# Attention with one head between its steps: minima of head h, then normalising h-1, scores of h+1, then turning h-1

## The chip, the cores and the metric

The kernel runs on one core of one Trainium2 chip. The metric is the device time of one execution in microseconds (us), lower is better. A core has TensorE (PE, matrix products; its weight loads are listed as PEld), VectorE (DVE), ScalarE (ACT), GpSimd (POOL) and SyncE (SP). Each engine takes its own instructions in the order in which they are written; engines wait for one another by semaphores, counters that one raises and another waits on.

## What is computed

A trunk of two residual layers over 512 tokens of width 1024, in float32. Layer 0 mixes tokens by a short gated convolution, layer 1 by multi-head latent attention; behind each mixer stands a SwiGLU feed-forward network, and a final RMS norm ends it. The change touches the attention of layer 1 alone: 16 heads, four blocks of 128 queries, and block j sees the first (j+1)*128 keys.

```python
for j in range(s // Q_BLOCK):
    q0, q1 = j * Q_BLOCK, (j + 1) * Q_BLOCK
    kend = q1
    logits = (jnp.einsum('bqhd,bkhd->bhqk', q_nope[:, q0:q1], k_nope[:, :kend])
              + jnp.einsum('bqhr,bkr->bhqk', q_rope[:, q0:q1], k_rope[:, :kend]))
    logits = logits.astype(jnp.float32) * scale
    mask = (pos[None, :kend] // CHUNK) <= (pos[q0:q1, None] // CHUNK)
    logits = jnp.where(mask[None, None], logits, NEG_INF)
    p = jax.nn.softmax(logits, axis=-1).astype(v.dtype)
    outs.append(jnp.einsum('bhqk,bkhd->bqhd', p, v[:, :kend]))
o = jnp.concatenate(outs, axis=1).reshape(bsz, s, MLA_HEADS * MLA_V)
return o @ w_o
```

## The kernel before

The program is written engine by engine, each with its own list of steps; nothing reorders them. The whole sequence stays on chip, transposed (features on partitions). Products of weights are made of three float32r products (high by high, high by low, low by high, lines 375 to 377). The stages follow one another: convolution, feed-forward, latent projections, attention, its output projection `mla_out`, feed-forward, final norm.

Within attention every head h goes through these steps:

- `q_head(h)` on TensorE makes the queries (6 products) and `rotate(h)` on VectorE applies the rotary table and writes them to `q_even` or `q_odd`. Both run ahead of the heads and end with head 15.
- `logits(h)` on TensorE (line 1552): scores of the four query blocks, into PSUM banks 0, 2 and 1, in three groups, each of which raises `s_prod`. There is one set of banks, so each group of `logits(h)` waits until `row_low(h-1)` has read its bank (`s_read`).
- `row_low(h)` on VectorE (line 1256): four instructions that scale and mask the scores, write them to `prob` and give each row's minimum of the negated score. `prob` has two buffers, by the head's parity, and so `row_low(h)` waits for `turn(h-2)` to be complete (`p_turned` at 3*(h-2)+3).
- `exponentials(h, 0)` and `(h, 1)` on ScalarE (line 852): exponentials in place, with sums of rows, for blocks 3 and 1, then 2 and 0 (`exp_done`).
- `normalise(h)` on VectorE (lines 1268 and 1272): reciprocals of the sums, and `prob` times them, for the same two halves. It ends with `p_ready`.
- `turn(h)` on TensorE (line 1613): ten transposes of 128x128 into PSUM banks 3 to 5. It waits for `p_ready` of h and, since those banks are single, for the copies of head h-1 (`pt_front`, `pt_back`).
- `front_copy(h)` on ScalarE (lines 861 and 863, two copies) and `back_copies(h)` on VectorE (line 1280, one copy) bring the transposed probabilities to SBUF, into `prob_T` or `prob_T2` by parity.
- `weigh(pair)` on TensorE (line 1629): 16 products with the values, for two heads at once; then `head_out(pair)` on ScalarE (line 867) and on VectorE (line 1284) splits the pair's output into `hid_hi` and `hid_lo`.

Two pieces of the next stage lie in between: `unit_hi` on ScalarE (line 350) and `unit_lo` on VectorE (line 359) split the first four weight blocks of `mla_out`, one in each pair 3 to 6.

The order is written by hand and goes by pairs i = 1 to 7. TensorE: logits(2i), turn(2i-1), logits(2i+1), weigh(i-1), turn(2i). VectorE: row_low(2i), back_copies(2i-1), normalise(2i), row_low(2i+1), normalise(2i+1), head_out(i-1), back_copies(2i). Here the minima of a head and its normalising stand next to each other on VectorE, while ScalarE makes the exponentials in between. After the pairs TensorE waits for the last `s_read` and goes on with products of `mla_out` over the finished chunks, with turn(15) and weigh(7) between them.

Of the kernel before, what the change touches and what calls it, by code (L numbers as in the profile page):

```python
# [91 lines left out]
def trunk_kernel(nc, w, consts, out):  # L92
# [7 lines left out]
    HEADS, NOPE, ROPE, VD = 16, 64, 32, 64  # L100
# [5 lines left out]
    PAIRS = HEADS // 2  # L106
# [24 lines left out]
    with ExitStack() as ctx:  # L131
# [211 lines left out]
        def unit_hi(eng, name, i, u):  # L343
            v, s, prev, nth = unit_numbers(name, i, u)
            _, n, width = source(name, i, u)
            eng.wait_ge(raw_in[s], nth * 16)
            if prev is not None:
                wait(eng, w_used, prev + 1)
            for dst, src in split_parts(name, s, n, width, wgt_hi):
                ins = nc.scalar.activation(dst, src, ACT.Copy)  # L350
            ins.then_inc(w_hi, 1)

        def unit_lo(eng, name, i, u):
            v, s, prev, nth = unit_numbers(name, i, u)
            _, n, width = source(name, i, u)
            wait(eng, w_hi, v + 1)
            for (dst, src), (hi, _) in zip(split_parts(name, s, n, width, wgt_lo),
                                           split_parts(name, s, n, width, wgt_hi)):
                ins = nc.vector.tensor_tensor(dst, src, hi.bitcast(F32), ALU.subtract)  # L359
            ins.then_inc(w_lo, 1)  # L360
# [284 lines left out]
        def _(sc):  # L645
# [200 lines left out]
            def exponentials(hd, n):  # L846

                par = hd % 2
                sc.wait_ge(s_read, 3 * hd + n + 2)
                for j in ((3, 1), (2, 0))[n]:  # L850
                    blk = prob[:, par, L_OFF[j]:L_OFF[j] + (j + 1) * P]
                    ins = nc.scalar.activation(blk, blk, ACT.Exp, bias=low[:, par, j:j + 1], scale=-1.0,
                                               accum_out=sums[:, par, j:j + 1])
                ins.then_inc(exp_done, 1)

            def front_copy(hd):

                sc.wait_ge(p_turned, 3 * hd + 1)
                if hd >= 2:
                    sc.wait_ge(pv_done, hd // 2)  # L860
                nc.scalar.activation(prob_Ts[hd % 2][:, 0, 0:512], ps[:, 3, :], ACT.Copy)
                sc.wait_ge(p_turned, 3 * hd + 3)
                nc.scalar.activation(prob_Ts[hd % 2][:, 0, 512:1024], ps[:, 4, :], ACT.Copy).then_inc(pt_front, 1)

            def head_out(pair):
                sc.wait_ge(pv_done, pair + 1)
                nc.scalar.activation(hid_hi[:, pair, :], ps[:, 6 + pair % 2, :], ACT.Copy).then_inc(o_hi, 1)

            exponentials(0, 0)
            exponentials(0, 1)  # L870
            exponentials(1, 0)
            exponentials(1, 1)
            front_copy(0)
            for i in range(1, PAIRS):
                exponentials(2 * i, 0)
                front_copy(2 * i - 1)
                exponentials(2 * i, 1)
                if 3 <= i < 7:
                    unit_hi(sc, "mla_out", 0, i - 3)
                exponentials(2 * i + 1, 0)  # L880
                exponentials(2 * i + 1, 1)
                head_out(i - 1)
                front_copy(2 * i)
            front_copy(HEADS - 1)
            head_out(PAIRS - 1)

# [36 lines left out]
        def _(ve):  # L923
# [313 lines left out]
            def rotate(hd):  # L1237

                if hd % GROUP == GROUP - 1:
                    ve.wait_ge(w_used, U0["q_up"] + hd // GROUP + 1)  # L1240
                else:
                    ve.wait_ge(q_prod, q_count(hd))
                nc.vector.tensor_tensor(q_Ts[hd % 2][:, hd // 2, :], ps[:, 6 + hd % 2, :], rope[:, :],
                                        ALU.mult).then_inc(q_out, 1)

            def row_low(hd):

                par = hd % 2
                if hd >= 2:
                    ve.wait_ge(p_turned, 3 * (hd - 2) + 3)  # L1250
                for n, j in enumerate((3, 1, 2, 0)):
                    W = (j + 1) * P
                    if n < 3:
                        ve.wait_ge(s_prod, 3 * hd + n + 1)
                    bank, col = {3: (0, 0), 1: (2, 0), 2: (1, 0), 0: (1, 384)}[j]
                    ins = nc.vector.tensor_tensor_reduce(
                        prob[:, par, L_OFF[j]:L_OFF[j] + W], ps[:, bank, col:col + W], mask[:, S - W:S],
                        -SCALE, 3.0e38, ALU.add, ALU.min, low[:, par, j:j + 1])
                    if n != 2:
                        ins.then_inc(s_read, 1)  # L1260

            def normalise(hd):

                par = hd % 2
                for n, js in enumerate(((3, 1), (2, 0))):
                    ve.wait_ge(exp_done, 2 * hd + n + 1)
                    two = slice(js[1], js[0] + 1, 2)
                    nc.vector.reciprocal(rec[:, par, two], sums[:, par, two]).then_inc(rec_done, 1)
                    ve.wait_ge(rec_done, 2 * hd + n + 1)
                    for j in js:  # L1270
                        blk = prob[:, par, L_OFF[j]:L_OFF[j] + (j + 1) * P]
                        ins = nc.vector.tensor_scalar(blk, blk, rec[:, par, j:j + 1], None, ALU.mult)
                ins.then_inc(p_ready, 1)

            def back_copies(hd):

                if hd >= 2:
                    ve.wait_ge(pv_done, hd // 2)
                ve.wait_ge(p_turned, 3 * hd + 2)
                nc.vector.tensor_copy(prob_Ts[hd % 2][:, 0, 1024:1280], ps[:, 5, 0:256]).then_inc(pt_back, 1)  # L1280

            def head_out(pair):
                ve.wait_ge(o_hi, pair + 1)
                nc.vector.tensor_tensor(hid_lo[:, pair, :], ps[:, 6 + pair % 2, :], hid_hi[:, pair, :].bitcast(F32),
                                        ALU.subtract).then_inc(o_lo, 1)
# [6 lines left out]
            for hd in range(3, 8):  # L1292
                rotate(hd)
            row_low(0)
            rotate(8)
            rotate(9)
            normalise(0)
            rotate(10)
            row_low(1)
            rotate(11)  # L1300
            normalise(1)
            back_copies(0)
            rotate(12)
            rotate(13)
            for i in range(1, PAIRS):
                row_low(2 * i)
                if i == 1:
                    rotate(14)
                back_copies(2 * i - 1)
                normalise(2 * i)  # L1310
                if i == 1:
                    rotate(15)
                row_low(2 * i + 1)
                if 3 <= i < 7:
                    unit_lo(ve, "mla_out", 0, i - 3)
                normalise(2 * i + 1)
                head_out(i - 1)
                back_copies(2 * i)
            back_copies(HEADS - 1)
            head_out(PAIRS - 1)  # L1320

# [44 lines left out]
        def _(pe):  # L1366
# [236 lines left out]
            def turn(hd):  # L1603

                pe.wait_ge(p_ready, hd + 1)
                if hd:
                    pe.wait_ge(pt_front, hd)
                    pe.wait_ge(pt_back, hd)
                for bs in ((0,), (2,), (1, 3)):
                    for b in bs:  # L1610
                        bank, col = {0: (3, 0), 2: (5, 0), 1: (4, 0), 3: (4, 384)}[b]
                        for j in range(b, TB):
                            ins = nc.tensor.transpose(ps[:, bank, col + (j - b) * P:col + (j - b + 1) * P],
                                                      prob[:, hd % 2, L_OFF[j] + b * P:L_OFF[j] + (b + 1) * P], ident)
                    ins.then_inc(p_turned, 1)
# [30 lines left out]
                q_head(hd)  # L1646
            logits(1)
            q_head(11)
            turn(0)
            q_head(12)  # L1650
            q_head(13)
            for i in range(1, PAIRS):
                logits(2 * i)
                if i == 1:
                    q_head(14)
                turn(2 * i - 1)
                if i == 1:
                    q_head(15)
                logits(2 * i + 1)
                weigh(i - 1)  # L1660
                turn(2 * i)

            def mla_out_products(u, ks):

# [1 line left out]
                chunk_products("mla_out", 0, u, ks, o_lo, 0)  # L1666

            pe.wait_ge(s_read, 3 * HEADS)
            mla_out_products(0, list(range(6)))
            turn(HEADS - 1)  # L1670
            mla_out_products(0, [6])
            mla_out_products(1, early)
            weigh(PAIRS - 1)
            mla_out_products(2, early)
            for u in range(3):
# [100 lines left out]
```

## Time and profile before

| | us |
|---|---|
| median of 3 runs | 1130.08 |
| lowest, highest | 1127.64, 1130.85 |
| the profiled execution, its own time | 1127.99 |
| its span in the profile | 1126.0 |
| TensorE busy | 1081.3 (96% of the span) |
| VectorE busy | 855.9 (76%) |
| ScalarE busy | 485.1 (43%) |

The profile is of one execution; times within it count from the start of the span, and 2.0 us of the execution's own time lie outside the span. Busy time of TensorE is modelled at the ends of products, which overlap a little; starts of instructions are the safer reading. "Idle before" is the time in which an engine stood still ahead of an instruction, with what ended it.

### The profile page before, as it was taken

To read this page: it belongs to the slowest core of one execution; us is meant where nothing else is said; L and a number is where in the kernel's file an instruction comes from. 1 tells how busy PE (TensorE), PEld (TensorE's weight loads), DVE (VectorE), ACT (ScalarE), POOL (GpSimd) and SP (SyncE) were. 2 spreads that over 40 slices of the span, in tenths; PEclk is the share of its full clock that TensorE was granted. 3 is DMA by queue.
4 is the path that set the end of the run, shared out by engine and by line. 5 is a ranking of instruction groups with operands and counts; after the bars stand their busy time and mean duration, and the time that the engine had idled before them with its cause. 6 is when DMAs were issued, how large, how long until landed. Compare 5 with 4: busy or idle time off the path is not lost. (4 is left out here: it accounts for less than half of the span.)

```text
span 1126.0 us, 19245 instructions
## 1 busy us (share of the span) xinstructions
PE 1081.3 (96%) x6630; PEld 956.1 (85%) x6630; DVE 855.9 (76%) x1316; ACT 485.1 (43%) x836; POOL 234.9 (21%) x179
## 2 busy tenths in 40 slices
PE   9999997799999999999999999977999999999997
PEld 7888886799999998888877766757999999988887
DVE  5855568899999997444578788388999999973443
ACT  6222233545445545222345577235454445452222
POOL 6000014333233320111200000143332333201110
PEclk9999999799999999999999999997999999999998
DMA  7333422123323333334232011021333233333321
GB/s 197 106 93 93 126 61 75 60 92 112 111 81 115 110 100 112 103 102 114 94 94 75 1 39 38 1 75 52 99 112 102 85 113 111 101 115 103 98 69 75
DMA packets 144040, 101.68 MB, mean 90 GB/s; under 512 B 3912, under 2 KB 142336, under 8 KB 144000
## 3 DMA queue, kind: packets, MB, share of 16 engines
q1 hardware_dynamic: 143648, 100.61, 29.2%
q0 software_dynamic: 320, 0.55, 0.2%
q8 instruction: 22, 0.36, 0.1%
q14 instruction: 18, 0.15, 0.0%
q10 hardware_dynamic: 32, 0.01, 0.0%
HBM read 99.06 MB, written 2.10 MB: 90 GB/s over the span
## 5 line engine op out<-in xcount | busy, mean ns | idle before, releaser
L375 PE MATMUL ps<-x_op_hi,op_w_hi 128*128 128x256 f32 x1232 | 353.5, 287 | 23.0 <-DVE x_op_lo L1021 22.1
L376 PE MATMUL ps<-x_op_lo,op_w_hi 128*128 128x256 f32 x1232 | 350.9, 285 | 0.0
L377 PE MATMUL ps<-x_op_hi,op_w_lo 128*128 128x256 f32 x1232 | 350.9, 285 | 0.0
L375 PEld LDWEIGHTS ps<-x_op_hi,op_w_hi 128*128 128x128 f32 x1232 | 239.0, 194 | 26.4 <-DVE x_op_lo L1021 22.5
L376 PEld LDWEIGHTS ps<-x_op_lo,op_w_hi 128*128 128x128 f32 x1232 | 239.0, 194 | 0.6 <-issue 0.5
L377 PEld LDWEIGHTS ps<-x_op_hi,op_w_lo 128*128 128x128 f32 x1232 | 238.9, 194 | 0.0
L375 PE MATMUL ps<-hid_hi,wgt_hi 128*128 128x512 f32 (+1 forms) x550 | 212.3, 386 | 4.2 <-DVE wgt_lo L359 4.2
L359 DVE TENSOR_TENSOR wgt_lo<-raw,wgt_hi 128x1024 fp32r<-128x1024 f32 (+4 forms) x131 | 137.6, 1066 | 101.9 <-ACT wgt_hi L350 100.5
L377 PE MATMUL ps<-hid_hi,wgt_lo 128*128 128x512 f32 (+1 forms) x550 | 210.1, 382 | 0.0
L376 PE MATMUL ps<-hid_lo,wgt_hi 128*128 128x512 f32 (+1 forms) x550 | 210.1, 382 | 0.0
L350 ACT ACTIVATE wgt_hi<-raw 128x1024 fp32r<-128x1024 f32 (+4 forms) x131 | 107.0, 831 | 151.0 <-PE ps L377 149.4
L595 POOL TENSOR_TENSOR sq<-xT 128x512 f32 (+1 forms) x36 | 38.2, 1062 | 560.4 <-DVE xT L1009 320.6
L510 DVE TENSOR_TENSOR op_w_lo<-w_sum,op_w_hi 128x512 fp32r<-128x512 f32 x176 | 135.2, 787 | 0.0
L505 ACT ACTIVATE op_w_hi<-w_sum 128x512 fp32r<-128x512 f32 x176 | 106.7, 623 | 66.1 <-PE ps L377 27.3
L610 POOL TENSOR_TENSOR w_sum<-pair_raw 128x512 f32<-128x512 f32 x44 | 68.9, 1565 | 271.6 <-DMA pair_raw<-in_ffn_w_up 145.5
L375 PEld LDWEIGHTS ps<-hid_hi,wgt_hi 128*128 128x128 f32 x550 | 103.7, 189 | 25.1 <-issue 5.4
L377 PEld LDWEIGHTS ps<-hid_hi,wgt_lo 128*128 128x128 f32 x550 | 103.8, 189 | 20.2
L376 PEld LDWEIGHTS ps<-hid_lo,wgt_hi 128*128 128x128 f32 x550 | 103.9, 189 | 19.6 <-issue 0.2
L510 DVE TENSOR_TENSOR op_w_lo<-pair_raw,op_w_hi 128x512 fp32r<-128x512 f32 x132 | 95.9, 727 | 2.7 <-ACT op_w_hi L505 2.7
L375 PE MATMUL ps<-xg_hi,wgt_hi 128*128 128x512 f32 x232 | 92.1, 397 | 0.2 <-DVE c_r L961 0.2
L377 PE MATMUL ps<-xg_hi,wgt_lo 128*128 128x512 f32 x232 | 90.4, 390 | 0.0
L376 PE MATMUL ps<-xg_lo,wgt_hi 128*128 128x512 f32 x232 | 90.3, 389 | 0.0
(161 smaller groups left out, 1319.3 us busy)
## 6 DMA issues: line engine op xcount, KB each, us to landing
pair_raw<-in_ffn_w_gate SPq DMA_DIRECT2D x22, 1024.0 KB, 5.1
pair_raw<-in_ffn_w_up SPq DMA_DIRECT2D x22, 1024.0 KB, 5.1
raw<-in_conv_w_in SPq DMA_DIRECT2D x24, 512.0 KB, 3.8
raw<-in_ffn_w_down SPq DMA_DIRECT2D x32, 384.0 KB, 3.3
raw<-in_ffn_w_down SPq DMA_DIRECT2D x32, 320.0 KB, 2.9
raw<-in_conv_w_out SPq DMA_DIRECT2D x8, 512.0 KB, 3.7
raw<-in_mla_w_o SPq DMA_DIRECT2D x8, 512.0 KB, 3.8
x_nat<-in_x SPq DMA_DIRECT2D x4, 512.0 KB, 6.9
```

What stands on the lines that cost most here:

```text
L350: ins = nc.scalar.activation(dst, src, ACT.Copy)
L359: ins = nc.vector.tensor_tensor(dst, src, hi.bitcast(F32), ALU.subtract)
L375: nc.tensor.matmul(acc, wh, xh, start=first, stop=False)
L376: nc.tensor.matmul(acc, wh, xl, start=False, stop=False)
L377: return nc.tensor.matmul(acc, wl, xh, start=False, stop=last)
L505: nc.scalar.activation(wide(op_w_hi, p), op_source(par, p), ACT.Copy).then_inc(op_hi, 1)
L510: nc.vector.tensor_tensor(wide(op_w_lo, p), op_source(par, p), wide(op_w_hi, p).bitcast(F32), ALU.subtract).then_inc(op_lo, 1)
L595: nc.gpsimd.tensor_tensor(sq[:, :], xT[:, ds(m, 1), :].rearrange("p a s -> p (a s)"), xT[:, ds(m, 1), :].rearrange("p a s -> p (a s)"), AL ...
L610: nc.gpsimd.tensor_tensor(wide(w_sum, 0), b["A21"], b["A22"], ALU.add).then_inc(sum_done, 1)
```

## The change

Only the order of steps in attention is changed, on three engines; every instruction, buffer and semaphore stays, with the same waits.

- VectorE, for h from 2 to 15: row_low(h), [head_out of pair (h-4)/2 for even h from 4], back_copies(h-2), normalise(h-1), [unit_lo for h = 5, 7, 9, 11].
- TensorE, for h from 1 to 14: logits(h+1), [q_head(h+12) for h up to 3], [weigh of pair (h-3)/2 for odd h from 3], turn(h-1).
- ScalarE, for h from 0 to 15: front_copy(h-2), [head_out for even h from 4], exponentials(h, 0), exponentials(h, 1), [unit_hi for h = 4, 6, 8, 10].
- Behind the loop TensorE has weigh(6), six chunks of `mla_out` block 0, turn(14), six chunks of block 1, turn(15), one chunk of each, weigh(7).

```diff
-            for i in range(1, PAIRS):
-                exponentials(2 * i, 0)
-                front_copy(2 * i - 1)
-                exponentials(2 * i, 1)
...
+            for hd in range(HEADS):
+                if hd >= 2:
+                    front_copy(hd - 2)
+                if hd >= 4 and hd % 2 == 0:
+                    head_out((hd - 4) // 2)
+                exponentials(hd, 0)
+                exponentials(hd, 1)
+                if hd in (4, 6, 8, 10):
+                    unit_hi(sc, "mla_out", 0, (hd - 4) // 2)
+            front_copy(HEADS - 2)
+            head_out(PAIRS - 2)
             front_copy(HEADS - 1)
             head_out(PAIRS - 1)
...
+            for hd in range(2, HEADS):
+                row_low(hd)
+                if hd < 4:
+                    rotate(hd + 11)
+                elif hd % 2 == 0:
+                    head_out((hd - 4) // 2)
+                back_copies(hd - 2)
+                normalise(hd - 1)
+                if hd == 3:
                     rotate(15)
-                row_low(2 * i + 1)
-                if 3 <= i < 7:
-                    unit_lo(ve, "mla_out", 0, i - 3)
-                normalise(2 * i + 1)
-                head_out(i - 1)
-                back_copies(2 * i)
+                if hd in (5, 7, 9, 11):
+                    unit_lo(ve, "mla_out", 0, (hd - 5) // 2)
+            back_copies(HEADS - 2)
+            normalise(HEADS - 1)
+            head_out(PAIRS - 2)
             back_copies(HEADS - 1)
             head_out(PAIRS - 1)
...
-            for i in range(1, PAIRS):
-                logits(2 * i)
-                if i == 1:
-                    q_head(14)
-                turn(2 * i - 1)
-                if i == 1:
-                    q_head(15)
-                logits(2 * i + 1)
-                weigh(i - 1)
-                turn(2 * i)
+            for hd in range(1, HEADS - 1):
+                logits(hd + 1)
+                if hd < 4:
+                    q_head(hd + 12)
+                if hd >= 3 and hd % 2:
+                    weigh((hd - 3) // 2)
+                turn(hd - 1)
...
             pe.wait_ge(s_read, 3 * HEADS)
+            weigh(PAIRS - 2)
             mla_out_products(0, list(range(6)))
+            turn(HEADS - 2)
+            mla_out_products(1, list(range(6)))
             turn(HEADS - 1)
             mla_out_products(0, [6])
-            mla_out_products(1, early)
+            mla_out_products(1, [6])
             weigh(PAIRS - 1)
```

VectorE in pair 4, before: the weight block, normalise(9), head_out(3), back_copies(8) and the first instruction of row_low(10). The names are those of the program; "waits" lists semaphores.

```order
L359 TENSOR_TENSOR wgt_lo<-raw,wgt_hi 128x1024 [waits w_hi]
L1268 RECIPROCAL small<-small 128x2 [waits exp_done]
L1272 TENSOR_SCALAR prob<-prob,small 128x512 [waits rec_done]
L1272 TENSOR_SCALAR prob<-prob,small 128x256
L1268 RECIPROCAL small<-small 128x2 [waits exp_done]
L1272 TENSOR_SCALAR prob<-prob,small 128x384 [waits rec_done]
L1272 TENSOR_SCALAR prob<-prob,small 128x128
L1284 TENSOR_TENSOR hid_lo<-ps,hid_hi 128x512 [waits o_hi]
L1280 COPY prob_T<-ps 128x256 [waits p_turned,pv_done]
L1256 ISA prob,small<-ps,mask 128x512 [waits s_prod,p_turned]
```

The last row waits for turn(8), whose normalise(8) stands a whole head further up in this queue. VectorE after, in the step of head 8 (lines are those of the changed kernel): head_out(2), back_copies(6), normalise(7), and the first instruction of row_low(9).

```order
L1280 TENSOR_TENSOR hid_lo<-ps,hid_hi 128x512 [waits o_hi]
L1276 COPY prob_T<-ps 128x256 [waits p_turned,pv_done]
L1264 RECIPROCAL small<-small 128x2 [waits exp_done]
L1268 TENSOR_SCALAR prob<-prob,small 128x512 [waits rec_done]
L1268 TENSOR_SCALAR prob<-prob,small 128x256
L1264 RECIPROCAL small<-small 128x2 [waits exp_done]
L1268 TENSOR_SCALAR prob<-prob,small 128x384 [waits rec_done]
L1268 TENSOR_SCALAR prob<-prob,small 128x128
L1252 ISA prob,small<-ps,mask 128x512 [waits s_prod,p_turned]
```

The last row waits for turn(7), and normalise(7), which turn(7) needs, now stands directly ahead of it.

TensorE before, from the end of weigh(2): turn(6), logits(8), turn(7), and the start of logits(9).

```order
L1629 MATMUL ps<-prob_T,v_nat 64x128
L1629 MATMUL ps<-prob_T_101,v_nat 64x128
L1613 MATMUL ps<-ident,prob 128x128 [waits pt_back,pt_front,p_ready]
L1613 MATMUL ps<-ident,prob 128x128 x9
L1552 MATMUL ps<-k_T,q_even 128x512 [waits s_read,q_out]
L1552 MATMUL ps<-k_T,q_even 128x256 [waits s_read]
L1552 MATMUL ps<-k_T,q_even 128x384 [waits s_read]
L1552 MATMUL ps<-k_T,q_even 128x128
L1613 MATMUL ps<-ident,prob 128x128 [waits pt_back,pt_front,p_ready]
L1613 MATMUL ps<-ident,prob 128x128 x9
```

TensorE after, from the same weigh(2): turn(6), logits(9), turn(7), and the start of logits(10).

```order
L1622 MATMUL ps<-prob_T,v_nat 64x128
L1622 MATMUL ps<-prob_T_101,v_nat 64x128
L1606 MATMUL ps<-ident,prob 128x128 [waits pt_back,pt_front,p_ready]
L1606 MATMUL ps<-ident,prob 128x128 x9
L1545 MATMUL ps<-k_T,q_odd 128x512 [waits s_read,q_out]
L1545 MATMUL ps<-k_T,q_odd 128x256 [waits s_read]
L1545 MATMUL ps<-k_T,q_odd 128x384 [waits s_read]
L1545 MATMUL ps<-k_T,q_odd 128x128
L1606 MATMUL ps<-ident,prob 128x128 [waits pt_back,pt_front,p_ready]
L1606 MATMUL ps<-ident,prob 128x128 x9
```

The scores that stand between two turns are now one head further ahead of them.

## Rows read from the trace of the kernel before

**Rows 1.** Busy by stretch: span, then PE, PEld, DVE, ACT, POOL, clock, DMA.

```profile
615.79:714.12 98.33, 93.13 (x508) 64.70 (x506) 72.94 (x260) 59.76 (x171) 0.00 (x0) 1.00 0.09 27
659.54:669.91 10.37, 9.14 (x54) 6.03 (x53) 8.89 (x33) 7.92 (x23) 0.00 (x0) 1.00 0.17 51
```

**Rows 2.** Waits between 615 and 715 us: total, times, longest.

```profile
DVE small L1268 <- ACT prob L852: 10.5, 15, 1.0
...
PE ps L1613 <- DVE prob_T L1280: 5.2, 5, 1.2
```

**Rows 3.** Timeline of PE, pair 4: start, duration, what, idle before and releaser.

```profile
659.54 2.32 PE L1552 MATMUL ps<-k_T,q_even 128*128 128x512 f32 x8
663.09 1.28 PE L1613 MATMUL ps<-ident,prob 128*128 128x128 f32 x10 [1.23 <-DVE prob_T L1280]
664.21 2.32 PE L1552 MATMUL ps<-k_T,q_odd 128*128 128x512 f32 x8
666.46 2.37 PE L1629 MATMUL ps<-prob_T,v_nat 128*64 128x512 f32 x16
668.77 1.31 PE L1613 MATMUL ps<-ident,prob 128*128 128x128 f32 x10
669.91 2.32 PE L1552 MATMUL ps<-k_T,q_even 128*128 128x512 f32 x8
```

**Rows 4.** Timeline of DVE, end of pair 3 and pair 4.

```profile
659.21 1.22 DVE L359 TENSOR_TENSOR wgt_lo<-raw,wgt_hi 128x1024 fp32r<-128x1024 f32 x1
660.34 0.16 DVE L1268 RECIPROCAL small<-small 128x2 f32<-128x2 f32 x1
...
661.93 0.68 DVE L1284 TENSOR_TENSOR hid_lo<-ps,hid_hi 128x512 fp32r<-128x512 f32 x1
662.53 0.41 DVE L1280 COPY prob_T<-ps 128x256 f32<-128x256 f32 x1
662.86 0.68 DVE L1256 CUSTOM_DVE_ANT_0 prob<-ps,mask 128x512 f32<-128x512 f32 x1
...
664.50 0.42 DVE L1280 COPY prob_T<-ps 128x256 f32<-128x256 f32 x1
...
667.21 0.17 DVE L1268 RECIPROCAL small<-small 128x2 f32<-128x2 f32 x1 [0.99 <-ACT prob L852]
```

**Rows 5.** Timeline of ACT, pair 5: exponentials, head_out, front_copy.

```profile
669.01 0.72 ACT L852 ACTIVATE prob<-prob,small 128x512 f32<-128x512 f32 x1 [0.89 <-DVE small L1256]
...
671.21 0.57 ACT L867 ACTIVATE hid_hi<-ps 128x512 fp32r<-128x512 f32 x1
671.68 0.58 ACT L861 ACTIVATE prob_T<-ps 128x512 f32<-128x512 f32 x1
```

**Rows 6.** Timeline of all engines at turn(15): turn and the second front copy.

```profile
705.17 1.26 PE L1613 MATMUL ps<-ident,prob 128*128 128x128 f32 x10
...
706.46 0.60 ACT L863 ACTIVATE prob_T<-ps 128x512 f32<-128x512 f32 x1
```

**Rows 7.** Timeline at q_head(14): its end (the next step's start) and rotate(14).

```profile
632.98 1.25 PE L1613 MATMUL ps<-ident,prob 128*128 128x128 f32 x10
...
633.18 0.69 DVE L1243 TENSOR_TENSOR q_even<-ps,rope 128x512 f32<-128x512 f32 x1 [0.62 <-PE ps L377]
```

**Rows 8.** Busy by stretch, columns as in group 1: stretches with gaps on PE.

```profile
600.00:610.00 10.00, 7.66 (x33) 5.75 (x32) 8.59 (x13) 6.84 (x13) 0.00 (x0) 1.00 0.07 20
740.00:750.00 10.00, 6.76 (x27) 5.18 (x26) 9.21 (x9) 3.66 (x5) 6.26 (x6) 0.91 0.14 41
750.00:760.00 10.00, 5.83 (x27) 4.74 (x25) 8.80 (x12) 4.29 (x8) 2.96 (x3) 0.84 0.18 64
```

**Rows 9.** Timeline of PE: the gaps within those stretches, and q_head(13).

```profile
603.08 0.50 PE L1594 MATMUL ps<-wgt_hi,hid_hi 128*128 128x512 f32 x1 [2.34 <-DVE v_nat L1168]
...
628.07 0.39 PE L375 MATMUL ps<-hid_hi,wgt_hi 128*128 128x512 f32 x1
...
629.43 2.32 PE L1552 MATMUL ps<-k_T,q_even 128*128 128x512 f32 x8
...
747.42 0.47 PE L375 MATMUL ps<-hid_hi,wgt_hi 128*128 128x512 f32 x1 [3.24 <-DVE wgt_lo L359]
```

More of the change, by code:

```diff
@@ L867, in head_out @@
                 nc.scalar.activation(hid_hi[:, pair, :], ps[:, 6 + pair % 2, :], ACT.Copy).then_inc(o_hi, 1)
[L869 to L873, printed above, removed]
-            for i in range(1, PAIRS):
-                exponentials(2 * i, 0)
-                front_copy(2 * i - 1)
-                exponentials(2 * i, 1)
-                if 3 <= i < 7:
-                    unit_hi(sc, "mla_out", 0, i - 3)
-                exponentials(2 * i + 1, 0)
-                exponentials(2 * i + 1, 1)
-                head_out(i - 1)
-                front_copy(2 * i)
+            for hd in range(HEADS):
[9 more added lines that the diff above has]
+            head_out(PAIRS - 2)
             front_copy(HEADS - 1)
@@ L1294, in _ @@
             row_low(0)
[L1295 to L1298, printed above, removed]
+            for hd in range(8, 11):
+                rotate(hd)
             row_low(1)
             rotate(11)
-            normalise(1)
-            back_copies(0)
             rotate(12)
-            rotate(13)
-            for i in range(1, PAIRS):
-                row_low(2 * i)
-                if i == 1:
-                    rotate(14)
-                back_copies(2 * i - 1)
-                normalise(2 * i)
-                if i == 1:
-                    rotate(15)
-                row_low(2 * i + 1)
-                if 3 <= i < 7:
-                    unit_lo(ve, "mla_out", 0, i - 3)
-                normalise(2 * i + 1)
-                head_out(i - 1)
-                back_copies(2 * i)
+            normalise(0)
+            for hd in range(2, HEADS):
[7 more added lines that the diff above has]
+                if hd == 3:
+                    rotate(15)
+                if hd in (5, 7, 9, 11):
[3 more added lines that the diff above has]
+            head_out(PAIRS - 2)
             back_copies(HEADS - 1)
@@ L1648, in _ @@
             q_head(11)
-            turn(0)
             q_head(12)
-            q_head(13)
-            for i in range(1, PAIRS):
-                logits(2 * i)
-                if i == 1:
-                    q_head(14)
-                turn(2 * i - 1)
-                if i == 1:
-                    q_head(15)
-                logits(2 * i + 1)
-                weigh(i - 1)
-                turn(2 * i)
+            for hd in range(1, HEADS - 1):
[5 more added lines that the diff above has]
+                turn(hd - 1)
             def mla_out_products(u, ks):
```

## The prediction, made before the changed kernel ran

> **What bounds the kernel now.** I read the busy times by stretch first, then the waits of attention, then the timelines of its engines. TensorE is busy 96% of the span, so the end moves by whatever idle time TensorE gains or loses. The change reorders attention only, from logits(0) to the end of weigh(7): 98.33 us with TensorE busy 93.13 and the granted clock at 1.00 (the 2.4 GHz level) [rows 1]. Its products are the same after the change, so what counts is their idle time. Of that the list of waits has 5.2 us in 5 pieces, all ahead of a turn, and all ended by back_copies on VectorE [rows 2]. Four are of the kind of pair 4: turn(7) starts 1.23 us late, since VectorE came to back_copies(6) only at 662.53, behind normalise(7) and head_out [rows 3, 4]. VectorE itself loses 10.5 us in 15 waits for exponentials [rows 2], because a head's normalising follows so soon on its minima; the largest is 0.99 us [rows 4]. A pair that carries a weight block takes 10.37 us, of which TensorE needs 9.14 [rows 1].
>
> **The prices, step by step.** From start to next start, where nothing is waited for. On TensorE logits take 664.21 to 666.46 = 2.25 us, weigh 2.31, a turn 663.09 to 664.21 = 1.12 [rows 3], a q_head about 1.4 (1.36 from 628.07 to 629.43) [rows 9]. On VectorE row_low takes 662.86 to 664.50 = 1.64, back_copies 0.33, head_out 0.60, normalise 660.34 to 661.93 = 1.59, unit_lo 1.13 [rows 4]. On ScalarE four exponentials take 669.01 to 671.21 = 2.20 and head_out 0.47 [rows 5].
> The way from engine to engine: a back copy that started at 662.53 let turn(7) start at 663.09, 0.56 after its start, or 0.23 after its 0.33 [rows 3, 4]; I take 0.23 for normalise to turn too. A turn is seen complete 1.29 us after its start (705.17 to 706.46) [rows 6], which is 0.17 behind its 1.12. VectorE has no such row for a turn; rotate(14) started 0.20 behind the end of its q_head [rows 7], which would give 1.32.
>
> **What the change removes.** normalise(h-1) now stands a whole head behind row_low(h-1), so the exponentials, 2.20 us, are long done: the 10.5 us of VectorE's waits go. back_copies(h-2) stands before normalise(h-1), so the 5.2 us of TensorE's waits for it go as well: -5.2 us on the path.
>
> **What it adds.** There are two buffers of prob, and row_low(h+1) writes the one that turn(h-1) reads. In the new order VectorE ends step h with normalise(h-1), and its next instruction is row_low(h+1). Turn(h-1) cannot start before normalise(h-1) is done, and row_low(h+1) cannot start before turn(h-1) is done: VectorE stands still for the whole turn. Queued behind row_low(h+1) are all its later steps, and TensorE's logits(h+2) wait for it as well, since there is one set of score banks. The two engines take turns where before they overlapped. Before, normalise(2i) and the row_low(2i+2) that needed its turn had row_low(2i+1), normalise(2i+1), head_out and back_copies(2i) between them, and normalise(2i-1) had more still ahead of row_low(2i+1).
>
> I write R for the start of row_low(h), and follow TensorE. The end of the turn before lies 0.17 ahead of R. logits(h+1) need the first of the four minima: it takes 0.68 [rows 4], and the way to TensorE I put at 0.15 from its end (copy ended 662.94, turn began 663.09 [rows 3, 4]), so R+0.83. That is an idle piece of 0.17 + 0.83 = **1.00 us ahead of every logits**. Before there was no such piece. No row shows TensorE waiting for this semaphore; the lower bound is 0.17 + 0.60 + 0.15 = 0.92 (the minimum without its tail, as head_out's step), the upper 0.17 + 0.83 + 0.23 = 1.23, if the weight load too comes behind the wait. I take 1.00, nearest to the row of the same instruction.
> - Odd h: logits to R+3.08, weigh to R+5.39. normalise(h-1) was done at 1.64 + 0.33 + 1.59 = R+3.56, so the turn starts at once and row_low(h+1) starts at 5.39 + 1.29 = R+6.68. unit_lo (1.13) ends at R+4.69 and is hidden.
> - Even h from 4: VectorE needs 1.64 + 0.60 + 0.33 + 1.59 = 4.16, and 0.23 more to TensorE: the turn starts at R+4.39. TensorE was free at R+3.08, so **1.31 us idle**, and row_low(h+1) starts at R+5.68.
> A pair takes 6.68 + 5.68 = 12.36 us, against 10.37 before with a weight block and about 9.14 without. ScalarE has some 8 us of work in it [rows 1] and does not bound it: its front_copy(h-2) is done by about R+1.0, head_out by R+1.5, ahead of VectorE's own head_out at R+1.64.
>
> **The edges.** Step 2: q_head(14) fills the gap (0.83 + 2.25 + 1.4 = 4.48 against 4.39), so no wait before turn(1). Step 3: weigh(0) waits for rotate(15), which starts 0.20 behind q_head(15) at R+4.68 and takes 0.60 and 0.23 more, R+5.51, against R+4.48: 1.03 us. The end: after turn(13) comes weigh(6), which waits for the last minima and for back_copies(13), at R+1.64+0.56 = 2.20, so with the 0.17 a wait of 2.37 us. Turn(14) lies behind weigh(6) and six chunks and waits for nothing. Turn(15) is followed by only two chunks (about 1.4 us) instead of eight before weigh(7): 1.12 + 1.4 = 2.5 us after its start, and its second front copy ends at 1.29 + 0.60 = 1.89 [rows 6], so it is covered with 0.4 us to spare.
>
> **The sum.** Thirteen logits (3 to 15) at 1.00 = 13.0; six turns (heads 3, 5, ... 13, in steps 4 to 14) at 1.31 = 7.9; step 3 1.0; the end 2.4: together 24.3 us of idle time, less the 5.2 of before = **+19.1 us**. On the profiled execution, 1127.99, that is 1147.1. It lies 2.1 below the median, and the median is what is compared: 1130.1 + 19.1 = **1149.2 us**. The stages behind start with products that only wait for weights loaded long before, and their gaps hang on what TensorE hands over, so they give nothing back.
> The bounds: the 13 pieces from 0.92 to 1.23 move the sum by -1.0 to +3.0; the four ways across engines in the 6 turns by about 0.6 either way; the median of three lay within a spread of 1127.64 to 1130.85. So 1145 to 1154.
>
> **Rivals.**
> 1. The clock falls. TensorE would be busy in 75% of a pair (9.14 of 12.36). For it: from 740 to 750 us it was busy 6.76 of 10 and the granted clock was 0.91, from 750 to 760 5.83 and 0.84 [rows 8]. Against it: there a gap of 3.24 us had come before, while from 600 to 610 us a gap of 2.34 left it at 1.00, busy 7.66 [rows 8, 9], and the gaps here are 1.0 to 1.3, one 2.4. If it fell, the 93.13 us of work would take 9.2 us more at 0.91 and 17.7 more at 0.84: 1158 to 1167. Chance 7%. The Trainium skill, TensorE: Matmul & The Clock Gate, section A second HAM failure mode: psum-queue depth-cycling, speaks for this rival: it reports a kernel that walks through PSUM banks where short idle pieces between groups of products made the clock go back and forth between its two levels. By that rule the time is this rival's; the row of 600 to 610 does not agree with it, nor do the five idle pieces of attention itself at 1.00.
> 2. VectorE alone sets the pace: if scores and weigh overlapped with it in both kinds of step, a pair would be 4.39 + 1.29 in even and 3.79 + 1.29 in odd steps, 10.76, which over six pairs is 9.6 us less: about 1140. Against it: weigh stands ahead of the turn in TensorE's queue and waits for nothing before it. Chance 6%.
> 3. The other side, faster: the wait for the turn costs nothing and only the removals count. It decides at VectorE's queue between normalise(h-1) and row_low(h+1): with 0.23 + 1.29 = 1.52 us of other work there the wait would vanish on VectorE's side. Only unit_lo, 1.13, stands there, in four of the steps, and the scores' wait for the minima stays. The price would be -5.2: 1124.9. Chance 2%, and 2% for a mixture that ends within 0.3% (3.4 us; about what a measurement can tell from no change).
> That the order isn't what it says can be left out: the queues show the steps in the new places.
>
> **How the numbers follow.** The forecast 1149.2, with 1145 to 1154 as its own range, has 83%; the clock 7%, VectorE's pace 6%, same 2%, faster 2%. The forecast's range by itself leaves out less than 2 in 10, so it stands. Faster 0.02, same 0.02, slower 0.83 + 0.07 + 0.06 = 0.96.
>
> **What would show it.** In the changed profile: TensorE's idle time ahead of logits, ended by the minima, 13 to 14 times about 1.0 us; idle ahead of six turns, ended by normalise, about 1.3; VectorE's idle ahead of row_low ended by a turn, near 1.5 us in even steps and near 3 in odd ones (6.68 - 3.56, less the weight block); its waits for exponentials gone; attention's stretch near 117.5 us instead of 98.3 with the clock at 1.00; pairs of 12.4 us. A pair at 10.8 speaks for rival 2, a clock under 1.00 for rival 1. The forecast is wrong if row_low starts before the turn has ended.

## The result and the profile after

The changed kernel takes **1153.03 us** in the median of 6 runs (1150.09 to 1154.46), against 1130.35 for the kernel before (6 runs, 1127.64 to 1130.94). The ratio is 1.02, with an interval of 1.0185 to 1.0216: 22.7 us slower. The forecast was 1149.2, with 1145 to 1154; its +19.1 us is 3.6 short of this.

The profiled execution has a span of 1151.5 us, 25.5 more than before. Its waits in attention and behind it, with their total, how often they occur and the longest (line 1606 is turn, 1252 row_low, 1545 logits, 1268 normalise, 1276 back_copies):

```profile
DVE prob L1252 <- PE ps L1606: 29.1, 14, 3.8
...
PE ps L1545 <- DVE small L1252: 11.5, 13, 0.9
...
PE ps L1606 <- DVE prob L1268: 6.4, 6, 1.1
...
PE ps L1622 <- DVE prob_T L1276: 2.4, 1, 2.4
```

None of these rows was there before; the two of [rows 2] are gone. VectorE now waits for every turn from turn(0) to turn(13). TensorE waits for the minima ahead of 13 scores, for normalise ahead of six turns, and once for a back copy, ahead of weigh(6). TensorE through heads 7 to 9 (start, duration, what, idle before and what ended it), to be read beside [rows 3]:

```profile
662.02 2.39 PE L1545 MATMUL ps<-k_T,q_odd 128*128 128x512 f32 x8 [0.88 <-DVE small L1252]
665.47 1.31 PE L1606 MATMUL ps<-ident,prob 128*128 128x128 f32 x10 [1.06 <-DVE prob L1268]
667.67 2.40 PE L1545 MATMUL ps<-k_T,q_even 128*128 128x512 f32 x8 [0.88 <-DVE small L1252]
669.99 2.37 PE L1622 MATMUL ps<-prob_T,v_nat 128*64 128x512 f32 x16
672.30 1.31 PE L1606 MATMUL ps<-ident,prob 128*128 128x128 f32 x10
674.49 2.40 PE L1545 MATMUL ps<-k_T,q_odd 128*128 128x512 f32 x8 [0.88 <-DVE small L1252]
```

From the scores at 662.02 to the next of the same kind at 674.49 a pair takes 12.47 us, against 10.37 before and 12.36 in the sum. VectorE in the same place:

```profile
661.17 0.69 DVE L1252 CUSTOM_DVE_ANT_0 prob<-ps,mask 128x512 f32<-128x512 f32 x1 [3.68 <-PE ps L1606]
...
664.80 0.61 DVE L1268 TENSOR_SCALAR prob<-prob,small 128x384 f32<-128x384 f32 x2
...
666.82 0.69 DVE L1252 CUSTOM_DVE_ANT_0 prob<-ps,mask 128x512 f32<-128x512 f32 x1 [1.40 <-PE ps L1606]
...
673.65 0.69 DVE L1252 CUSTOM_DVE_ANT_0 prob<-ps,mask 128x512 f32<-128x512 f32 x1 [2.04 <-PE ps L1606]
```

This is the exchange of turns that was forecast. The row_low at 661.17 (head 8) ends in a normalise at 664.80 to 665.41, the turn starts at 665.47, and 1.35 us after the turn the next row_low starts. The 2.04 of the odd step is what the weight block (unit_lo) leaves of the wait.

A second thing shows in two rows of TensorE, where operations that occur elsewhere last longer:

```profile
653.56 4.03 PE L1545 MATMUL ps<-k_T,q_even 128*128 128x512 f32 x8 [0.88 <-DVE small L1252]
...
719.06 4.53 PE L1622 MATMUL ps<-prob_T,v_nat 128*64 128x512 f32 x16 [2.36 <-DVE prob_T L1276]
```

Scores took 4.03 instead of 2.39, and weigh(6) 4.53 instead of 2.37, with the four products behind it a little longer too. The granted clock in stretches around them (span; busy time of PE, PEld, DVE, ACT, POOL; granted clock; DMA share; GB/s; the first is attention from logits(0) to the end of weigh(7)):

```profile
616.12:738.58 122.46, 101.35 (x508) 67.27 (x506) 72.37 (x260) 62.91 (x171) 0.00 (x0) 0.96 0.08 22
...
650.00:660.00 10.00, 8.05 (x39) 4.64 (x38) 5.99 (x21) 4.85 (x14) 0.00 (x0) 0.83 0.13 37
660.00:715.00 55.00, 42.12 (x226) 26.67 (x225) 38.27 (x142) 36.60 (x98) 0.00 (x0) 1.00 0.11 33
715.00:725.00 10.00, 7.25 (x30) 4.17 (x31) 3.90 (x17) 3.48 (x10) 0.00 (x0) 0.67 0.01 2
```

Around them the clock is below 1.00, between them it is 1.00, so products ran for some microseconds at the lower of the clock's two levels, 1.2 GHz. Below, such a piece is called a slow stretch. Before, the same stage stood at 1.00 throughout [rows 1].

**Where the time went.** Attention, from logits(0) to what follows weigh(7), took 122.5 us instead of 98.3, 24.1 more. Of the rest of the span's 25.5, 0.3 lies ahead of attention and 1.1 behind it. The slow stretches are priced from start to next start: 653.56 to 657.52 less the 2.32 of the scores at 667.67 = 1.64, then 719.06 to 723.52 less 2.31 = 2.15, and about 0.75 in the four products behind, 4.5 in all. What is left, 19.6, is the exchange of turns, for which the sum had 19.1.

### The profile page after: what moved, and what is told of

The parts are those of the page before. It is cut to its first block and busy times, and to the rows that moved or that the text cites. A ratio compares the mean times of both kernels' runs of the same rounds, so it can differ in the third digit from the quotient of the medians.

```text
span 1151.5 us, 19246 instructions
## 1 busy us (share of the span) xinstructions
PE 1086.7 (94%) x6630; PEld 955.1 (83%) x6630; DVE 856.3 (74%) x1316; ACT 488.4 (42%) x836; POOL 233.8 (20%) x179
## 5 line engine op out<-in xcount | busy, mean ns | idle before, releaser
L375 PEld LDWEIGHTS ps<-hid_hi,wgt_hi 128*128 128x128 f32 x550 | 104.1, 189 | 25.5 <-issue 5.7
```

The source lines that it names most:

```text
L375: nc.tensor.matmul(acc, wh, xh, start=first, stop=False)
```

## Experiments

The kernel before was run beside each group of four: its median was 1130.18 us beside third_buffer, filler, copy_behind and copy_ahead (all on one chip), and 1128.83 beside the other four (on another chip). It was 1130.35 beside the changed kernel. So a kernel of the second group looks up to 1.5 us better against the changed kernel's 1153.03 than it is, and the third column below, the distance from the kernel before in the same group, is the safer one. Several executions of one kernel spread over 1.4 to 4.4 us. Attention, in the profile of one execution, is taken from the start of logits(0) to the start of the product behind weigh(7).

| kernel | median, us | less the kernel before beside it | attention in its profile | slow stretches there |
|---|---|---|---|---|
| before | 1130.35 | | 98.3 | 0 |
| changed | 1153.03 | 22.7 | 122.5 | 2 |
| third_buffer | 1138.19 | 8.0 | 107.1 | 1 |
| third_buffer_old_order | 1129.85 | 1.0 | 98.3 | 0 |
| out_last | 1147.32 | 18.5 | 116.0 | 1 |
| third_buffer_out_last | 1126.23 | -2.6 | 94.6 | 0 |
| copy_behind | 1151.93 | 21.8 | 121.2 | 2 |
| copy_ahead | 1156.26 | 26.1 | 126.6 | 4 |
| filler | 1160.94 | 30.8 | 129.9 | 0 |
| filler_short | 1149.79 | 21.0 | 117.9 | 0 |

### A third buffer for the probabilities

The changed kernel with three buffers in place of two; the minima, sums and reciprocals have three as well.

```diff
+        prob3, _, e = place("prob3", [P, 1, L_COLS], F32, TMP)
+        probs = [prob[:, 0, :], prob[:, 1, :], prob3[:, 0, :]]
...
-                par = hd % 2
-                if hd >= 2:
-                    ve.wait_ge(p_turned, 3 * (hd - 2) + 3)
+                par = hd % 3
+                if hd >= 3:
+                    ve.wait_ge(p_turned, 3 * (hd - 3) + 3)
```

> The changed kernel with a third buffer for prob and for its minima, sums and reciprocals (by the head modulo 3), so that row_low(h) waits for turn(h-3) instead of turn(h-2); the order of all steps stays. My theory (VectorE stands still for each turn because row_low(h+1) follows normalise(h-1) directly and there are two buffers): VectorE's waits for a turn, 29.1 us in 14 times, go, and so do the 13 waits of TensorE for the minima. By the same steps as in the prediction, with this one wait taken out, a pair of heads falls from 12.4 us to 10.7, since VectorE then waits in every even step for head_out on ScalarE, which comes behind weigh: attention about 12.6 us shorter, 1140.4 with the same losses by the clock and 1135.6 without them. Rival A (the loss lies in the order of the copies and the scores, not in the buffer): within 2 us of the changed kernel, 1153. Rival B (the wait for the turn is the whole loss): as before the change or better, 1125 to 1130.

Measured: 1138.19 us, ratio 1.0067 (1.0051 to 1.0084), 14.8 us below the changed kernel. That is between the two figures of the theory (with and without losses by the clock) and far from both rivals. Attention is 15.3 us shorter in the profile; 2.8 of that is the clock (one slow stretch of 1.7 us in place of 4.5), so the buffer is worth 12.5, and the theory had 12.6. Waits of the profile (line 1610 turn, 1272 normalise, 1284 head_out):

```profile
DVE hid_lo L1284 <- ACT hid_hi L871: 18.1, 7, 4.3
...
PE ps L1610 <- DVE prob L1272: 9.9, 6, 1.7
```

VectorE's waits ahead of row_low for a turn and TensorE's for the minima are gone. What is left is the second chain of the new order: in even steps VectorE has head_out ahead of back_copies and normalise, head_out needs ScalarE's half, and that needs weigh, which now stands later. The pair takes 10.82 us (turns at 661.08 and 671.90 in the rows of TensorE), 10.7 by the sum. One slow stretch remained, at weigh(6), 4.07 us long.

### The third buffer in the old order

```diff
-                if hd >= 2:
-                    ve.wait_ge(p_turned, 3 * (hd - 2) + 3)
+                if hd >= 3:
+                    ve.wait_ge(p_turned, 3 * (hd - 3) + 3)
```

The base here is the kernel before; the rest of the edit is as above.

> The kernel before, its order untouched, with the third buffer of prob and of the small sums. Theory: in the order before no row_low waits for a turn, so a further buffer changes nothing: 1130.2, within 1. Rival (the buffer is a gain by itself, whatever the order): as third_buffer_out_last, 1127.

Measured: 1129.85 us (11 runs), ratio 1.0000 (0.9991 to 1.0009). Its waits have the same row as [rows 2], under another line number:

```profile
PE ps L1617 <- DVE prob_T L1284: 5.2, 5, 1.2
```

Attention takes 98.3 us in both profiles. So the buffer is no gain by itself; of the two orders it matters only in the one where row_low follows directly on the normalise of the head whose buffer it wants.

### head_out behind normalise

```diff
-                elif hd % 2 == 0:
-                    head_out((hd - 4) // 2)
                 back_copies(hd - 2)
                 normalise(hd - 1)
+                if hd >= 4 and hd % 2 == 0:
+                    head_out((hd - 4) // 2)
```

First on the changed kernel with its two buffers:

> The changed kernel with only VectorE's head_out moved behind normalise(h-1), two buffers as before. Theory: the turn of each even step comes earlier by head_out's 0.6 us, and head_out lies in VectorE's wait for the turn: six times 0.6, 3.6 us, so 1149.4; the wait for each turn itself stays, 14 times. Rival (head_out's place is the main loss, not the buffer): near 1140 or less.

Measured: 1147.32 us, ratio 1.0146 (1.0129 to 1.0164). Its distance from the kernel before is 18.5 us, 4.2 less than the changed kernel's 22.7 (the plain difference of the two medians, 5.7, holds the 1.5 us by which the second group ran lower). TensorE's row for the turn of an even step:

```profile
664.68 1.31 PE L1606 MATMUL ps<-ident,prob 128*128 128x128 f32 x10 [0.47 <-DVE prob L1268]
```

The wait ahead of it fell from 1.06 to 0.47, the 0.6 of the theory, in six steps 3.6 us. In the two profiles attention is 6.5 us shorter: 3.5 by this and the rest by the clock, since one stretch was slow (weigh(6), 3.46 us, 1.6 us lost with the products behind it) instead of two that lost 4.5.

Then with the third buffer as well:

> third_buffer, and VectorE's head_out moved in each even step from in front of back_copies(h-2) to behind normalise(h-1). In third_buffer VectorE still waited 18.1 us in 7 times for head_out on ScalarE, and the turns of the even steps came 1.66 us late for it. Theory: those waits leave the path, a pair takes what TensorE needs, about 9.1 us; attention is 9.9 us shorter than in third_buffer by the same steps, and up to 1.7 more where the clock doesn't fall: 1126.5 to 1128.5, which is 2 to 4 us below the kernel before. Rival (VectorE's work of 7.7 to 8.9 us for a pair or ScalarE's 8 already bind): a pair of 9.5 to 10, 1131 to 1134.

Measured: **1126.23 us** (5 runs, 1124.21 to 1126.66), ratio 0.9961 (0.9947 to 0.9975): a little faster than the kernel before, by 0.4% in the ratio and by 2.6 us, 0.2%, between the medians, and just below what was expected. Attention is 94.6 us in the profile, 3.75 shorter than before. TensorE goes through the pair without a wait:

```profile
655.30 2.32 PE L1549 MATMUL ps<-k_T,q_odd 128*128 128x512 f32 x8
657.46 1.25 PE L1610 MATMUL ps<-ident,prob 128*128 128x128 f32 x10
658.55 2.33 PE L1549 MATMUL ps<-k_T,q_even 128*128 128x512 f32 x8
660.81 2.38 PE L1626 MATMUL ps<-prob_T,v_nat 128*64 128x512 f32 x16
663.11 1.31 PE L1610 MATMUL ps<-ident,prob 128*128 128x128 f32 x10
664.26 2.32 PE L1549 MATMUL ps<-k_T,q_odd 128*128 128x512 f32 x8
```

664.26 less 655.30 is 8.96 us a pair, what TensorE's products need. So the new order is no worse than the old one when it has three buffers and head_out behind normalise; with two buffers it is slower with either place of head_out.

### Work put into the waits and in front of them

Eleven VectorE copies, one in each of the steps 4 to 14, first where VectorE waits for the turn:

```diff
                 normalise(hd - 1)
+                if 4 <= hd <= 14:
+                    nc.vector.tensor_copy(spare[:, :], mask[:, :])
```

> The changed kernel with one more VectorE copy of 128x512 (mask to a spare buffer, about 0.6 us) in each of the steps 4 to 14, directly behind normalise(h-1), where VectorE waits for the turn: 11 copies, 6.6 us of work. Theory: they cost nothing, since the waits there are 1.4 us in even steps and 2.0 in odd ones: 1153, within 1. Rival (VectorE's work as such sets the pace): 6.6 us more, 1159.6.

Measured: 1151.93 us, ratio 1.0197 (1.0177 to 1.0217), 1.1 below the changed kernel, within the spread of both. VectorE's rows show the copy inside the wait:

```profile
665.19 0.42 DVE L1308 COPY spare<-mask 128x512 f32<-128x512 f32 x1
666.67 0.69 DVE L1254 CUSTOM_DVE_ANT_0 prob<-ps,mask 128x512 f32<-128x512 f32 x1 [1.07 <-PE ps L1610]
```

The wait is 1.07 instead of 1.40, and row_low comes no later. The copy took 0.42 us, and 0.34 from its start to the next instruction's where nothing is waited for, not the 0.6 that I had put down for a 128x512 operation from rows that read PSUM. The 11 copies are thus 3.7 us of work and not 6.6. If VectorE's work as such set the pace, that would still have given 1156.7.

Then the same copies ahead of back_copies(h-2):

> The same 11 copies, but ahead of back_copies(h-2) and normalise(h-1), so in front of the turn. Theory: in the six even steps the chain row_low, head_out, back_copies, normalise, turn sets the pace and each copy costs its full 0.6 us, 3.6 us in all; in the five odd steps TensorE's scores and weigh cover it (the turn comes 1.8 us behind normalise there): 1156.6. Rival (VectorE's work as such): 6.6 us more, 1159.6, as for the copies behind. Rival (TensorE alone): nothing, 1153.

Measured: 1156.26 us, ratio 1.0234 (1.0217 to 1.0251), 4.3 above copy_behind in the same group. TensorE's row for an even turn:

```profile
665.84 1.31 PE L1610 MATMUL ps<-ident,prob 128*128 128x128 f32 x10 [1.40 <-DVE prob L1270]
```

The wait grew from 1.06 to 1.40, by 0.34, in six steps 2.0 us; the odd steps did not change. This is how far VectorE's chain, and not its amount of work, sets the pace. The other 2.3 us are not the copies' own time: this profile has four slow stretches (653.54, 680.85, 708.16, 724.14), that of copy_behind two. Whether the copies brought the two more about, by longer idle pieces, or chance did, is not shown. The total came out as expected (1156.6) by two errors that cancelled: the copy was cheaper, the clock dearer. By its total alone this run doesn't tell the theory from VectorE's work as such, which at the real price of a copy would give about the same; copy_behind and the rows do.

### Products that nothing reads, in TensorE's waits

```diff
+            def filler(pair, n):
+                pe.wait_ge(*((o_lo, pair - 1) if pair >= 2 else (q_out, HEADS)))
+                for _ in range(n):
+                    nc.tensor.matmul(ps[:, 6 + pair % 2, 0:128], ones[:, :], ones[:, :], start=True, stop=True)
...
+                if hd >= 4:
+                    filler((hd - 2) // 2, 8)
                 logits(hd + 1)
...
+                if hd >= 4 and hd % 2 == 0:
+                    filler((hd - 2) // 2, 8)
                 turn(hd - 1)
```

> The changed kernel with products of ones that nothing reads, into the PSUM bank of the next weigh: 8 of 128 columns (about 0.9 us) ahead of each of the logits(5) to logits(15), 8 ahead of the turn in even steps from 4, and 18 ahead of weigh(6). They lie in TensorE's waits. Theory (two short stretches at a granted clock of half, at logits(6) and at weigh(6), cost what my sum lacked, 4.8 us in the profiled execution, and come from TensorE's idle pieces): the granted clock stays at 1.00 through attention and the time is 3 to 5 us below the changed kernel, 1148 to 1150. Rival (those stretches have another cause, or they are noise of one execution): no gain, or up to 1 us slower by fillers that end behind the wait, 1153 to 1154.

Measured: 1160.94 us, ratio 1.0271 (1.0254 to 1.0288), 7.9 slower than the changed kernel: a miss. The fillers were too long:

```profile
662.59 1.95 PE L1647 MATMUL ps<-ones 128*128 128x128 f32 x16
664.37 2.32 PE L1545 MATMUL ps<-k_T,q_odd 128*128 128x512 f32 x8
```

Eight products lasted 1.78 us, not 0.9, since I had taken the 0.11 us of a transpose for them; in this profile each float32 product stands as two rows. They ran past the waits. No stretch was slow, but the total does not tell what the clock is worth, since the fillers themselves cost time. So it was run again with half of them.

> The filler run again with half the products: in filler each product of 128 columns in float32 took 0.22 us, twice what I had taken, so that 8 lasted 1.79 us and ran past the waits. Here 4 (0.9 us) stand ahead of each of the logits(5) to logits(15) and of the turn in even steps, and 9 (2.0 us) ahead of weigh(6), products of ones that nothing reads. Theory (the short stretches at half the clock come from TensorE's idle pieces and cost 1.6 us or more each, two to four in an execution): no product in attention at the half clock, and 3 to 5 us below the changed kernel: 1148 to 1150. Rival (noise, or another cause): 1153.

Measured: 1149.79 us (4 runs, 1148.74 to 1150.17), ratio 1.0173 (1.0157 to 1.0188). It is 3.2 below the changed kernel between the medians, but 1.7 by the distances from the kernel before beside each, and the two ratios' intervals just touch. TensorE, of the same steps as above:

```profile
662.28 2.39 PE L1545 MATMUL ps<-k_T,q_odd 128*128 128x512 f32 x8
664.51 1.06 PE L1647 MATMUL ps<-ones 128*128 128x128 f32 x8
665.74 1.31 PE L1606 MATMUL ps<-ident,prob 128*128 128x128 f32 x10 [0.17 <-DVE prob L1268]
666.88 1.06 PE L1647 MATMUL ps<-ones 128*128 128x128 f32 x8
667.93 2.40 PE L1545 MATMUL ps<-k_T,q_even 128*128 128x512 f32 x8
...
674.76 2.39 PE L1545 MATMUL ps<-k_T,q_odd 128*128 128x512 f32 x8
```

A pair is as long as in the changed kernel, 674.76 less 662.28 = 12.48 us, so the waits are the same, only filled. And the clock stays up, in the columns as above:

```profile
650.00:680.00 30.00, 29.49 (x184) 21.61 (x184) 21.34 (x78) 21.11 (x56) 0.00 (x0) 1.00 0.13 37
680.00:710.00 30.00, 29.66 (x181) 20.46 (x180) 20.92 (x79) 18.30 (x52) 0.00 (x0) 1.00 0.13 36
```

The cleanest comparison is attention itself: from 618.02 to 735.92 it takes 117.9 us with the clock at 1.00, against 122.5 in the changed kernel, 4.5 less, which is the price of the slow stretches worked out above. So the clock's losses in attention go when TensorE's idle pieces are filled. In the medians they are worth 1.7 to 3.2 us of the 22.7, and no closer than that, since other slow stretches come and go outside attention. One is behind the idle piece of 2.34 us at 603 us that the prediction leaned on. The row of before has the clock at 1.00 there [rows 8]; in filler_short it is this:

```profile
600.00:610.00 10.00, 7.67 (x27) 5.86 (x26) 7.13 (x12) 7.33 (x14) 0.00 (x0) 0.83 0.00 0
```

The changed kernel and filler_short have the same program up to there. Four of the ten profiles (before, changed, the two with copies) have 1.00 there, and from its end to logits(0) pass 12.6 to 12.7 us; the other six have 0.83 and 14.2 to 14.3 us. So after the same idle piece the clock fell in some executions and not in others.

## Why the prediction came out as it did

- **The mechanism** was right: "VectorE stands still for the whole turn". 14 waits for turns stand in the profile, and taking the buffer conflict away took 14.8 us away, 12.5 of it in attention apart from the clock.
- **13 idle pieces ahead of logits at 1.00**: 13 were found. From the turn's start to the next scores is 665.47 to 667.67 = 2.20, less 1.12 for the turn: 1.08. The two ways across were each a little longer, 1.35 instead of 1.29 from turn to row_low, 0.85 instead of 0.83 from row_low to scores. The row of rotate(14), with 1.32, would have been the better one.
- **Six turns at 1.31**: six were found, at 665.47 less 662.02 less the 2.32 of scores = 1.13 us. The row_low of that step starts at 661.17, so the turn came at R+4.30 instead of R+4.39: the way from normalise to the turn is 0.14 and not the 0.23 of a back copy. And TensorE was free at R+3.17 instead of R+3.08, since scores took 2.32 behind an idle piece instead of 2.25.
- **Step 3 at 1.0 and the end at 2.4**: 0.87 (at 643.40, for rotate(15)) and 2.36 in the column of idle time.
- **What was removed**: TensorE's waits for back_copies ahead of the turns and VectorE's for exponentials are gone, as said.
- **The pair**: 12.36 predicted, 12.47 measured. The exchange as a whole: 19.1 predicted, 19.6 measured. That this is so close is partly luck: 13 pieces longer by 0.08 and 13 scores longer by 0.07 add 1.9 us, and six turns shorter by 0.18 take 1.1 away. The prediction's own sign, attention near 117.5 us with the clock at 1.00, was met by filler_short with 117.9; the changed kernel had 122.5 at 0.96.
- **The clock** was a rival of its own, all or nothing, at 7%. The step that failed is there: the gaps of 1.0 to 1.3 us were judged too small because a single gap of 2.34, and five pieces in attention, had left the clock at 1.00. The single gap was one execution's chance: behind the same gap the clock fell in six of the ten profiles. In attention the clock fell for short stretches, two in this execution at 4.5 us together. This term was put at nothing in the sum. The profiled execution is 25.4 us above the one before, 6.3 more than the 19.1: 4.5 of that is the clock in attention, 0.5 the exchange, 1.4 lies outside attention. The medians, where 3.6 was missing, can't be divided so. The rival's price of 9 to 18 us was too high by far, since it took the fall to last for the whole stage. The page of the Trainium skill that was cited beside it (TensorE: Matmul & The Clock Gate, A second HAM failure mode: psum-queue depth-cycling) reports a kernel in which frequent short idle pieces between groups of products made the clock go back and forth. This trace agrees: the granted clock fell and rose again twice, with a mean of 0.96 over attention.
- **Rival 2**, VectorE's chain alone, and **rival 3**, only removals, did not occur with two buffers. With three buffers and head_out moved, the time falls to 1126.2, 2.6 below the kernel before; rival 3 had 5.2 below, 1124.9.

Behind attention 1.1 us of the profiled difference has no cause that was tried. A wait of 1.30 us of TensorE for VectorE's operand at 797.30, which the trace of before does not have, may be part of it. The other eight profiles took 412.1 to 412.4 us from the end of attention, against 411.9 before and 412.9 in the changed kernel, so this part moves by some tenths whatever the order.

## What to carry to other kernels

When steps on one engine are set apart by hand, look for each step at the nearest later step in the same queue that waits for its consumer. If the two become neighbours, the engine stands still for the consumer's whole time, and distance between producer and consumer must be paid for with one more buffer. Count too what idle pieces do to TensorE: here a stage full of gaps of about 1 us lost up to 4.5 us more by the clock in one execution. And don't take a clock of 1.00 behind one gap in one profile as proof that such a gap is harmless.

## What the runs showed of the hardware

- The granted clock fell for short stretches in a stage where TensorE's products need 9.14 us of each 12.47 us pair. The idle pieces ahead of the slow scores were at most 1.1 us (1.4 in copy_ahead), and 0.9 to 2.4 us ahead of a slow weigh(6). Each slow stretch cost 1.6 to 2.9 us. With the waits filled the same stage stood at 1.00. How many slow stretches there were differed: two, two and four in the profiles of the changed kernel, copy_behind and copy_ahead.
- After one and the same idle piece of 2.34 us, with the same work around it, the granted clock of the next microseconds was 1.00 in four profiles and 0.83 (600 to 610 us) in six, and the six lost 1.5 us by it.
- A 128x512 float32 copy on VectorE from SBUF to SBUF took 0.42 us, where operations of that size that read PSUM took 0.68.
- A float32 product of 128 columns took 0.22 us (eight in 1.78), a transpose of the same size 0.11 (ten in 1.12).
- From the start of a turn to the start of the VectorE instruction that waits for it passed 1.35 us, of which the ten transposes are 1.12.
